# Row-tiled selects for the per-head scales, and a new order of sums in the down-projection of a two-block transformer kernel

## What is computed

```python
# second network, mixer: every head of q and k is normalised by its own root mean square
q_mla = rms_norm_2(q_mla, lp["g_qn_mla"])                                   # 8 heads of 96
q_gqa = rms_norm_2(q_g.reshape(b, l, GQA_HEADS, GQA_DIM), lp["g_qn_gqa"])   # 8 heads of 64
k_mla = rms_norm_2(jnp.concatenate([k_nope, k_rope], axis=-1), lp["g_kn_mla"])
k_gqa = rms_norm_2(k_g.reshape(b, l, GQA_KV_HEADS, GQA_DIM), lp["g_kn_gqa"])
# forgetting attention, first network, layer 0
logits = logits + F_b[..., :, None] - F[..., None, :]
# mLSTM, first network, layer 1
D = jnp.where(causal, b[..., :, None] - b[..., None, :] + ic[..., None, :], NEG_INF)
# every FFN: causal depthwise convolution between two projections
h = causal_depthwise_conv(xn @ w_up, conv_w) + conv_b
g, u = jnp.split(h, 2, axis=-1)
return (jax.nn.gelu(g) * u) @ w_down
```

## Time and profile before

| | |
|---|---|
| Runs of the kernel | 2566.29, 2571.61, 2571.93 us |
| Median | 2571.61 us |
| Profiled execution, its own time | 2566.29 us |
| Profiled execution, span from first to last instruction | 2564.4 us |
| Mean granted TensorE clock | 0.998 |
| PE busy | 2510.8 us, 98% |
| DVE, POOL, ACT busy | 49%, 24%, 21% |
| DMA | 334.93 MB, mean 131 GB/s |

### The profile page before, as it was taken

One profiled execution on the slowest core, in us unless ns is written; L12 is line 12 of the kernel. 1 busy time (PEld: TensorE's weight loads), 2 busy tenths in 40 slices (PEclk: granted clock), 3 DMA queues, 4 the chain that ended last, 5 costly groups with the idle time before them and its releaser, 6 DMA issues.

```text
span 2564.4 us, 36872 instructions
## 1 busy us (share of the span) xinstructions
PE 2510.8 (98%) x14120; PEld 2041.6 (80%) x14120; DVE 1246.9 (49%) x2513; ACT 533.2 (21%) x1167; POOL 624.7 (24%) x520
## 2 busy tenths in 40 slices
PE   8989999999999999999999999999999999999999
PEld 6857889986699998644667766888888875899999
DVE  3034168751325886314645763645551236434774
ACT  1131122112212221212531001222200223212220
POOL 0020135200212530001432221232240004332543
PEclk9999999999999999999999999999999999999999
DMA  6322264643234565110013662221222130244442
GB/s 236 132 99 106 91 222 180 259 177 144 103 132 170 199 226 229 70 68 25 1 58 136 233 254 93 80 97 66 111 91 78 66 117 1 95 153 165 164 189 107
DMA packets 39827, 334.93 MB, mean 131 GB/s; under 512 B 3856, under 2 KB 10128, under 8 KB 22416
## 3 DMA queue, kind: packets, MB, share of 16 engines
q1 hardware_dynamic: 39696, 333.11, 34.8%
HBM read 332.04 MB, written 1.05 MB: 130 GB/s over the span
## 4 chain that ended last, share of the span: by engine, by line
PE 90%; DVE 4%; DMA 2%; POOL 2%; issue 2%; ACT 0%; DVEq 0%; SPq 0%; POOLq 0%; ACTq 0%
PE PS L756 24%; PE PS L556 20%; PE PS L1016 6%; PE PS L2677 6%; PE PS L1507 5%; PE PS L1689 4%; PE PS L2718 4%; PE PS L1325 3%; PE PS L1677 2%; PE PS L2249 2%; PE PS L1348 2%; PE PS L1336 2%; DMA slot<-in_weights 1%; PE PS L431 1%; PE PS L737 1%
## 5 line engine op out<-in xcount | busy, mean ns | idle before, releaser
L556 PE MATMUL PS<-XN,slot 128*128 128x256 f32 (+1 forms) x1184 | 296.8, 411 | 0.8 <-DVE XN L495 0.8
L756 PE MATMUL PS<-SQ,slot 128*128 128x128 f32 (+1 forms) x1984 | 294.2, 301 | 1.2 <-DVE slot L852 1.2
L556 PEld LDWEIGHTS PS<-XN,slot 128*128 128x128 f32 x1184 | 224.5, 190 | 69.9 <-issue 42.5
L756 PEld LDWEIGHTS PS<-SQ,slot 128*128 128x128 f32 x1984 | 268.1, 191 | 14.2 <-DVE slot L852 1.4
L756 PE MATMUL PS<-XN,slot 128*128 128x128 f32 (+1 forms) x1664 | 250.0, 301 | 0.0
L556 PE MATMUL PS<-arena,slot 128*128 128x256 f32 x1088 | 238.3, 381 | 9.6 <-DMA slot<-in_weights 9.6
L556 PEld LDWEIGHTS PS<-arena,slot 128*128 128x128 f32 x1088 | 208.0, 191 | 38.6 <-issue 10.1
L756 PEld LDWEIGHTS PS<-XN,slot 128*128 128x128 f32 x1664 | 226.1, 192 | 10.7
L879 DVE SCALAR_TENSOR_TENSOR arena<-PS,small,arena 128x255 f32<-128x255 f32 (+2 forms) x352 | 174.7, 543 | 46.1 <-ACT arena L823 43.3
L823 ACT ACTIVATE arena<-PS,small 128x256 f32<-128x256 f32 (+1 forms) x176 | 105.1, 616 | 374.8 <-DVE PS L912 241.1
L1466 POOL TENSOR_SCALAR probs<-probs,pair_rec 128x512 f32<-128x512 f32 (+2 forms) x64 | 88.0, 1380 | 228.0 <-DVE pair_rec L1434 228.0
(11 more groups left out here) (283 smaller groups left out, 3745.1 us busy)
## 6 DMA issues: line engine op xcount, KB each, us to landing
slot<-in_weights SPq DMA_DIRECT2D x85, 2048.0 KB, 7.7
arena<-in_mod SPq DMA_DIRECT2D x96, 512.0 KB, 3.4
slot<-in_weights SPq DMA_DIRECT2D x16, 2816.0 KB, 9.8
slot<-in_weights SPq DMA_DIRECT2D x24, 1536.0 KB, 6.7
slot<-in_weights SPq DMA_DIRECT2D x6, 1024.0 KB, 4.8
slot<-in_weights SPq DMA_DIRECT2D x2, 2176.0 KB, 8.7
arena<-in_c SPq DMA_DIRECT2D x3, 1024.0 KB, 10.7
small<-in_small SPq DMA_DIRECT2D x1, 2301.0 KB, 17.7
```

What stands on the lines that cost most here:

```text
L556: mm = pe.matmul(o, l, r, start=k == 0, stop=k == len(terms) - 1, skip_group_check=True)
L756: mm = pe.matmul(PS[:, bank, 0:h], lhs[:, k * P:(k + 1) * P], rhs(k), start=first and k == 0, stop=last and k == 3, skip_group_check=True)
```

## The change

One part replaces the selects. Two new constants, `spread_halves` (4 x 128 columns) and `spread_quarters` (2 x 128), hold for each of 8 rows the output partitions of its head, and stand at each of the four partition groups. A spread becomes one matmul over 8 rows with 128 columns. The forgetting attention's select takes 8 rows, the mLSTM's 4. The clearing on POOL, the setting of unused PSUM rows on DVE, and the waits for both go.

The other part is in the down-projection of `b0` and `b1`. PE takes p6 ahead of p7, with the ring of PSUM banks in that order. t3 moves from DVE to POOL (L1134). In `b1` alone, t1 moves on DVE from behind the up stage into it (right behind the last but one block's c21), and s3 of the first slab moves from DVE to POOL, ahead of the last `h`. POOL's sums of the second slab no longer wait for s4 of the first slab, but stand behind t3.

```diff
+    sizes["spread_halves"] = 4 * P
+    sizes["spread_quarters"] = 2 * P
...
-        def select(h, each=P):
-
-            return ident[:, h:h + 1].broadcast_to([P, each])
+        def select(n, h):
+
+            return ident[0:n, h:h + 1].broadcast_to([n, P])
...
                     .then_inc(*w_tick(s, VD, "c21", i, turn))
+                if early and turn is None and i == FM - 1:
+                    early(dve)
                 if s[0] == "a" and turn is not None:
                     if i == 0:
...
-        D_ORDER = ["p1", "p2", "p5", "p7", "p6", "p4", "p3"]
+        D_ORDER = ["p1", "p2", "p5", "p6", "p7", "p4", "p3"]
         D_RING = [4, 5, 6, 0, 2, 3, 1, 7]
...
-                pe.wait_ge(*of(d, "s3", p))
-                pe.wait_ge(*of(d, "t3"))
-                product("p7", s3, lambda k: d_tile(t3, k)).then_inc(*tick(TD, d, "p7", p))
                 pe.wait_ge(*of(d, "s2", p))
                 pe.wait_ge(*of(d, "t2"))
                 product("p6", a11, lambda k: d_tile(t2, k)).then_inc(*tick(TD, d, "p6", p))
                 lend(d_bank(p, "p5"), (d, "x12", p))
                 lend(d_bank(p, "p6"), (d, "u2", p))
+                pe.wait_ge(*of(d, "s3", p))
+                pe.wait_ge(*of(d, "t3"))
+                product("p7", s3, lambda k: d_tile(t3, k)).then_inc(*tick(TD, d, "p7", p))
                 pe.wait_ge(*of(d, "t4"))
                 product("p4", a22, lambda k: d_tile(t4, k)).then_inc(*tick(TD, d, "p4", p))
                 lend(d_bank(p, "p7"), (d, "u3", p))
...
                 Stream.slab += 1
 
+        def vector_down_first(dve, s, n):
+            h, d = n // 2, f"d{s}"
+            (b11, b12), _ = d_hidden(n)
+            dve.wait_ge(*of(s, "h", PAIRS - 1, "last"))
+            dve.tensor_tensor(d_token_sums(n)[0][0][2], b12, b11, ALU.subtract).then_inc(*tick(VD, d, "t1"))
+
         def vector_down_seven(dve, s, pairs, n, gate):
...
                 return dve.scalar_tensor_tensor(out=x, in0=src, scalar=gate(m, g if n > T else 0), in1=x, op0=ALU.mult,
                                                 op1=ALU.add)
 
-            (b11, b12), _ = d_hidden(n)
-            dve.wait_ge(*of(s, "h", PAIRS - 1, "last"))
-            dve.tensor_tensor(t1[0][2], b12, b11, ALU.subtract).then_inc(*tick(VD, d, "t1"))
+            if n > T:
+                vector_down_first(dve, s, n)
             for p in range(pairs):
-                slot, landed, value = d_slab(s, p)
-                a11, a12, a21, _ = d_quarters(slot)
+                slot, _, _ = d_slab(s, p)
+                a11, a12, _, _ = d_quarters(slot)
                 ps = {what: d_psum(p, what, h) for what in D_ORDER}
-                if p == 0 and n == T:
-                    dve.wait_ge(landed, value)
-                    dve.wait_ge(*of(d, "s1", p))
-                    dve.tensor_tensor(a21, a11, a21, ALU.subtract).then_inc(*tick(VD, d, "s3", p))
-                if p == 0:
-                    dve.wait_ge(*of(s, "h", FM - 1))
-                    for lo, hi, ap in t3:
-                        op = dve.tensor_tensor(ap, b22[:, lo:hi, :], b12[:, lo:hi, :], ALU.subtract)
-                    op.then_inc(*tick(VD, d, "t3"))
                 dve.wait_ge(*of(d, "p1", p))
                 dve.wait_ge(*of(d, "s1", p))
                 dve.wait_ge(*of(d, "s3", p))
                 dve.tensor_tensor(a11, D_S1[p % 2], a11, ALU.subtract).then_inc(*tick(VD, d, "s2", p))
                 if p == 0:
                     dve.wait_ge(*of(d, "t1"))
+                    dve.wait_ge(*of(s, "h", FM - 1))
                     dve.tensor_tensor(t2[0][2], b22, t1[0][2], ALU.subtract).then_inc(*tick(VD, d, "t2"))
                 add_to_x(p, 0, 0, ps["p1"]).then_inc(*tick(VD, d, "x11", p))
                 if p:
...
@@ -1123,14 +1123,16 @@
                 pool.wait_ge(*of(d, "p5", p - 2))
                 pool.wait_ge(*of(d, "s2", p - 2))
             pool.tensor_tensor(D_S1[p % 2], a21, a22, ALU.add).then_inc(*tick(GD, d, "s1", p))
-            if p == 0 and s == "b1":
-                return
             pool.wait_ge(*of(d, "s1", p))
             pool.tensor_tensor(a21, a11, a21, ALU.subtract).then_inc(*tick(GD, d, "s3", p))
 
         def gpsimd_down_seven(pool, s, pairs, n):
             d = f"d{s}"
-            pool.wait_ge(*of(d, "s4", 0))
+            (_, b12), (_, b22) = d_hidden(n)
+            pool.wait_ge(*of(s, "h", FM - 1))
+            for lo, hi, ap in d_token_sums(n)[2]:
+                op = pool.tensor_tensor(ap, b22[:, lo:hi, :], b12[:, lo:hi, :], ALU.subtract)
+            op.then_inc(*tick(GD, d, "t3"))
             for p in range(1, pairs):
                 gpsimd_down_sums(pool, s, p)
 
...
-                vector=lambda d: vector_up_seven(d, s, norm, segs),
+                vector=lambda d: vector_up_seven(d, s, norm, segs, (lambda e: vector_down_first(e, s, n))
+                                                 if early and n == T else None),
...
-                        sc.append((i, c0, c1, select(2 * t + i), row_of(0)[:, 0:c1 - c0], False, True))
+                        sc.append((i, c0, c1, select(8, 2 * t + i), rows[0:8, 0, 0:c1 - c0], False, True))
...
-                    dec.append((c0, c1, select(h), row_of(2)[:, 0:n], True, True))
+                    dec.append((c0, c1, select(4, h), rows[0:4, 2, 0:n], True, True))
...
-                add(tensor=tensor_lstm_gates, vector=vector_lstm_gates,
-                    gpsimd=lambda p: p.memset(row_of(2), 0.0).then_inc(*tick(GD, "lstm", "cleared")))
+                add(tensor=tensor_lstm_gates, vector=vector_lstm_gates)
                 add_log_sigmoid("lstm", add, C, tick, of, rows, 4, 3, ("lstmgate", "read", 0, 1), eps_col)
...
-                    dve.wait_ge(*of("lstm", "cleared"))
...
 
-            def vector_low(dve, s=s, l=l, nq=nq, q_dst=q_dst, hn=hn):
-                if nq < 512:
-                    for g in (1, 2):
-                        op = dve.memset(PS[32 * g:32 * g + 32, 7, nq:512], 1.0)
-                    op.then_inc(*tick(VD, hn, "unused_set"))
...
 
-            def tensor_spread(pe, name, t, hn=hn, tiles=tiles, bank_of=bank_of):
+            def sel_rows(name, t):
+                g, _, _, _, heads, _, _, _ = tiles[name, t]
+                r = slice(32 * g, 32 * g + 8)
+                return sm("spread_halves" if heads == 2 else "spread_quarters")[r, t * P:(t + 1) * P], r
+
+            def tensor_spread(pe, name, t, hn=hn, tiles=tiles, bank_of=bank_of, sel_rows=sel_rows):
                 bank = bank_of["S", name, t]
                 n = tiles[name, t][3]
-                g, _, _, _, heads, _, _, _ = tiles[name, t]
-                each = P // heads
+                lhs, r = sel_rows(name, t)
                 claim(pe, bank)
                 pe.wait_ge(*of(hn, "rstd"))
-                for i in range(heads):
-                    mm = pe.matmul(PS[each * i:each * (i + 1), bank, 0:n], select(32 * g + heads * t + i, each), RST[:, 0:n],
-                                   start=True, stop=True, skip_group_check=True)
-                mm.then_inc(*tick(TD, hn, "spread", name, t))
+                pe.matmul(PS[:, bank, 0:n], lhs, RST[r, 0:n], start=True, stop=True)\
+                    .then_inc(*tick(TD, hn, "spread", name, t))
                 lend(bank, (hn, "out", name, t))
 
             def vector_out(dve, name, t, hn=hn, ro=ro, tiles=tiles, bank_of=bank_of):
...
+    r, c = i[:, None] % 32, np.arange(4 * P)[None]
+    put("spread_halves", (c // 64 == r) * 1.0)
+    put("spread_quarters", (c[:, :2 * P] // 32 == r) * 1.0)
```

8 lines of the change are left out of this document (3 added, 5 removed).

## The result

The changed kernel takes 2606.83 us (median of 4 runs, 2600.36 to 2607.9) against 2569.63 for the kernel before (4 runs): ratio 1.0141, 95% interval 1.0118 to 1.0163, so 1.4% slower. Forecast were 2574 us, with 2561 to 2583 as the range. The profiled execution's span grew by 36.0 us, from 2564.4 to 2600.5.

A forecast was written before the change was run, and what follows sets the result against it. PE was taken to bound the kernel (busy 98% of the span). -7.0 - 2.9 + 1.4 + 8.6 + 2.5 = +2.6 gave 2568.9 us against the profiled execution, 2574.2 by the median of runs; range 2561 to 2583.

The forecast's parts named there:

- Forgetting attention: Forgetting attention's select, 128 to 8 rows among 64-row scores: mode changes as often as before, 0 (within 0.5 us).
- the +1.4 of the mLSTM: mLSTM decay units: entering and leaving a four-row piece costs about 0.35 us in each of four units, +1.4 us.
- Layer 0's heads, -7.0: First heads stage: spreads of a group run at once in four row groups, saving 7.0 us.
- a group at 1.05: Heads stages: a group of spreads takes 1.05 us instead of 3.79, 2.80 and 1.94.
- DVE's outputs as the next limit: First heads stage: DVE's outputs, 0.67 us each, take over; 2.5 of PE's 9.5 us saving becomes waiting on DVE.
- Rival C: Heads stages: row tiles of a group don't overlap, heads give nothing, 2584.1 us (2580.1 if two at a time); chance 0.18.
- Layer 1's heads, -2.9: Second heads stage: 15.0 us becomes 12.1 of DVE work without a gap, saving 2.9 us.
- b1, +8.6: b1's down stage: POOL's and DVE's sums take turns, so p4 starts at 2512.8 instead of 2504.26, +8.6 us.
- The lock and its turns: Down stages: POOL and DVE operations with two SBUF inputs exclude each other and alternate; in b1 the sequence takes 23.9 us.
- Rivals A and B: Down stages: A, lock costs little, DVE wins ties, 2565.5 us, chance 0.2; B, DVE and POOL side by side, 2561.3, chance 0.12.
- b0, +2.5: b0's down stage: t2 ends at 1885.8 and p6 starts there instead of p7 at 1883.34, +2.5 us.
- The other zeros: Larger constants at the start, POOL's clearing, the PSUM setting and their waits: nobody waited for them, 0.

The follow-up runs named there:

- second to fourth experiment: Against the kernel before: only the two selects, 8 and 4 rows (1.0049); only the 8-row spreads (1.0037); selects, decays and spreads over 32 rows (1.0093).
- fifth and sixth: Against the kernel before: merged spreads over all 128 rows with decays over 64 rows, ratio 0.9999; merged spreads over 64 rows, ratio 0.9981.

## Why the prediction was wrong

- **The step that failed** is one that the prediction didn't price: that PE's rate stays what it was while the selects and spreads get few rows. "Forgetting attention: the array changes mode as often as before: 0", and the +1.4 of the mLSTM, counted columns and changes of mode at the upper clock. Shown in its place: work in 32-row tiles in place of full-height work, whether 4, 8 or 32 rows are used (second to fourth experiment), brings the granted clock to half for 10 to 31 us; full-height spreads and 64-row spreads and decays bring no such stretch in the profiled executions (fifth and sixth; the forgetting attention's select was not tried over 64 rows). By what the chip goes stays open. By the table it cost 6.1 in the forgetting attention, 4.0 of the mLSTM's 5.4, 6.2 behind the first heads stage and 12.1 in and behind the second, each against its forecast: 28.4 of the 33.4 us between the forecast's +2.6 and the +36.0 of the profiled execution. No rival had it, so the range, 2561 to 2583, could not.
- **Layer 0's heads, -7.0**: the stage itself gave -6.7, and its steps (a group at 1.05, measured 1.13; DVE's outputs as the next limit, 0.20 waits at the rotations) are borne out. The scores then gave it back. Rival C, row tiles one after another, is refuted by 1.14 for four. The reading behind it was wrong: of the eight records of the earlier trace rows four are 64-row and four 32-row ones, so pairs of 32-row tiles were seen to overlap already, and at the upper clock.
- **The mLSTM's +1.4** was about right as a price of the change of mode: over 64 rows, at the upper clock, the decays cost +1.0.
- **Layer 1's heads, -2.9**: +9.2 with its scores; but for its first 4 us the stage was never seen at the upper clock.
- **b1, +8.6**: +7.3 between p1 and p4, and +8.6 to the end, since a short stretch at the lower clock lies right behind p4's start. That this equals the forecast is luck. The lock and its turns, in the order forecast, are right to within 0.6 in 23.9. Rivals A and B are refuted there. The ground given for it, that the two alternated "in every case of the trace", is wrong: in `b0` before, POOL's s1, issued at 1886.82, came behind three pieces of DVE's t4 (6.08).
- **b0, +2.5**: the wait for t2 was 2.16; t4 (0.75) and the short stretch (1.7) had been left out, and b0 came to +5.1.
- The other zeros (constants, clearing, PSUM setting, their waits) hold: no stage without one of the edits moved by more than 1.8.

The Trainium skill, "TensorE: Matmul & The Clock Gate", "Part 1: The HAM clock gate (the "warmup" mystery)", says that a clock gate follows how busy PE has been lately. By idle time alone the long stretches could not be: PE was busy 20.5 of 20.5 us in the first. The short ones behind waits of 2 to 3 us in the down stages agree with it.

## What to carry to other kernels

Before making matmuls smaller in rows, ask what the rest of the stage will be clocked at: here spreads in 1.14 us instead of 3.79 halved PE's rate in what followed, which gave back nearly all of the gain in layer 0 and more than it in layer 1. Look at the granted clock stage by stage, not only at its mean, and at that of every execution, not only of the one profiled. 64-row tiles cost far less of it than 32-row ones, but gained at most 0.2% here. Moving a two-input sum from DVE to POOL is no relief where both are in use: it takes twice as long (3.17 instead of 1.61), and the other engine waits for it.
